# Two memory attentions in a two-block transformer kernel: the root applied to the products, rotary tables computed earlier, latent rounds and weight splits reordered

## The chip, the cores and the metric

The kernel runs on one core of one Trainium2 chip. The metric is the device time of one execution in microseconds, from the hardware's own counters; lower is better. Before the change it takes 3033.23 us (median of 3 runs, 3032.83 to 3034.36).

## What is computed

512 tokens of width 1024 in float32 pass through a first block (state-space, gated recurrence and retention mixers, then a feed-forward) and a second block of two layers. The change touches three parts of the second block, cut here to what matters:

```python
def memory_attention(q_mem, mem, mem_norm_g, w_mem_kv, g_q, g_k):
    q = rms_norm(q_mem.reshape(b, s, MEM_HEADS, MEM_HEAD_DIM), g_q)
    k, v = jnp.split(rms_norm(mem, mem_norm_g) @ w_mem_kv, 2, axis=-1)
    k = rms_norm(k.reshape(b, m, MEM_HEADS, MEM_HEAD_DIM), g_k)
    ...
def mla_queries(h, w_in, g_q_lora, w_uq, g_q_nope, g_q_rope, cos, sin):
    ...
    q = (rms_norm(c_q, g_q_lora) @ w_uq).reshape(b, s, MLA_HEADS, QK_HEAD_DIM)
    q_nope = rms_norm(q[..., :QK_NOPE_DIM], g_q_nope)
    q_rope = apply_rope(rms_norm(q[..., QK_NOPE_DIM:], g_q_rope), cos, sin)
```

The queries of the second layer (the latent attention) are shown; its keys are normed and turned likewise. `rms_norm(mem, g) @ w` is (mem * g * root) @ w with one reciprocal root for each of the 256 memory tokens, so the root can also multiply the product. `cos` and `sin` depend on `positions` alone.

## The kernel before

**Tiling.** Activations lie transposed, 128 channels by 512 tokens to a tile. Weights come as a stream of panels of 128 x 1024 float32 (8 blocks of 128 x 128) in the fixed order of `weight_stream`. Each float32 value is split into a high and a low half; `three` (L661 to L665) makes each block product of three matmuls: high by high, low by high, high by low. A full panel is 24 matmuls of 512 columns; a panel on the 256 memory tokens is 24 of 256 columns.

**Who does what.** SyncE loads panels into four slots `raw`. ScalarE (ACT) makes the high half `w_hi` (L1343). VectorE (DVE, L1850) or, in the panel ranges `POOL_RUNS`, GpSimd (POOL, L622) makes the low half `w_lo`. There are two slots each of `w_hi` and `w_lo`, so the split of panel n+2 starts when panel n is done. Products land in four PSUM banks in turn and are drained by ACT (L1348) or by DVE (`scaled`, L1923); four more (AUX) serve the small steps.

**Order.** Each engine has its own hand-written list; semaphores join them. A waiting instruction holds up all behind it on its engine. The places of the change:

- *First layer* (`conv0`, `qm0`, `conv1`, `mem0`, `conv`): a short convolution of 18 panels with the memory attention woven in. DVE squares and sums the memory tokens (`memory_squares`, L1905 and L1906), multiplies gain and root in and splits (`memory_input`, L2503, L1855, L1856); ACT drains the four `mem0` products. DVE's list ends the stretch with three `w_lo` in a row, and does a part of the convolution (`conv_part(st, 3, 1, 3)`) before the norms of keys and queries.
- *Second layer, latent part* (`mla_in`, `ukv`, `uq`): the heads are normed in rounds of three tiles. A round r is: squares (ACT, L1391), `round_sums` (PE, L796), root (ACT, L1396), reciprocal (DVE, L2023), `round_spread` (PE, L808), three norms (DVE, L2028). Between them stand the `uq` products (`uq_gemm`), four panels for the memory (`mem1_gemm`), turned values (`v_turned_tiles`, L1209) and the rotary turn (`turn`, L2653 to L2655). DVE computes the angle and both rotary tables (L2623 to L2633) between `mla_in` and `ukv`; ACT then takes their sine.
- *Attention steps*: scores, maxima, exponentials, probabilities and values, two steps ahead, from `pair_scores(0)` on.

## Time and profile before

| | us |
|---|---|
| median of 3 runs | 3033.23 (3032.83 to 3034.36) |
| the profiled execution | 3031.66 |
| its span, first to last instruction | 3029.8 |
| PE busy | 2986.1 (99%) |
| DVE busy | 1831.4 (60%) |
| ACT busy | 944.1 (31%) |
| POOL busy | 233.0 (8%) |
| mean granted clock of TensorE | 0.995 |

The trace gives each instruction a start and a duration. Matmuls overlap, so a matmul's own duration says little; the distance from one start to the next is what it costs. In brackets stands how long the engine sat idle before a row and what ended the wait.

### The profile page before, as it was taken

How to read it: one execution, taken by the hardware profiler on the slowest of the kernel's cores; microseconds unless marked ns; L12 is line 12 of the kernel's file. 1: busy time of each engine (PE TensorE's matmuls, PEld its weight loads, DVE VectorE, ACT ScalarE, POOL GpSimd, SP SyncE). 2: the span in 40 equal slices, each digit the busy share in tenths (PEclk: the TensorE clock that was granted, in tenths of full speed). 3: DMA queues.
4: the chain of work that ended last, by engine and by line, in shares of the span. 5: the costliest groups of instructions: out<-in, count | busy, mean ns of one | idle time of the engine just before them, and what ended most of it. 6: DMA issues, size and time to landing. Idle time of an engine off the chain costs nothing.

```text
span 3029.8 us, 36196 instructions
## 1 busy us (share of the span) xinstructions
PE 2986.1 (99%) x13373; PEld 2419.6 (80%) x13373; DVE 1831.4 (60%) x2405; ACT 944.1 (31%) x1279; POOL 233.0 (8%) x107
## 2 busy tenths in 40 slices
PE   8999999999999999999999999999999998999999
PEld 7788788788888888888787888888888875688887
DVE  8896565667766556554577655446554477665532
ACT  4643642333222223222223322222222235322222
POOL 0043340000000000000032000003000022000000
PEclk9999999999999999999999999999999999999999
DMA  4222123223222322223332222332223321122232
GB/s 147 94 95 84 63 98 118 70 95 114 96 94 96 101 98 92 97 95 104 113 104 71 91 97 97 102 106 98 91 96 104 105 87 63 36 91 97 97 104 97
DMA packets 79305, 287.55 MB, mean 95 GB/s; under 512 B 8992, under 2 KB 9248, under 8 KB 78816
## 3 DMA queue, kind: packets, MB, share of 16 engines
q1 hardware_dynamic: 77904, 280.06, 27.8%
q0 software_dynamic: 1296, 6.03, 0.6%
q8 instruction: 73, 1.20, 0.2%
q14 instruction: 32, 0.26, 0.0%
HBM read 283.96 MB, written 2.10 MB: 94 GB/s over the span
## 4 chain that ended last, share of the span: by engine, by line
PE 84%; issue 10%; DVE 4%; POOL 2%; ACT 0%; DMA 0%; POOLq 0%; ACTq 0%
PE ps L663 26%; PE ps L665 26%; PE ps L664 26%; POOL w_lo L622 2%; PE ps L1051 1%; PE ps L1296 0%; PE ps L1259 0%; DVE w_lo L1850 0%; PE ps L832 0%; PE ps L726 0%; PE ps L840 0%; PE ps L1040 0%; ACT w_hi L1343 0%; PE ps L946 0%; PE ps L1262 0%
## 5 line engine op out<-in xcount | busy, mean ns | idle before, releaser
L1343 ACT ACTIVATE w_hi<-raw 128x1024 fp32r<-128x1024 f32 x524 | 554.5, 1058 | 1381.8 <-PE ps L665 1379.7
L663 PE MATMUL ps<-h_hi,w_hi 128*128 128x512 f32 (+1 forms) x2379 | 935.6, 393 | 6.7 <-issue 2.0
L665 PE MATMUL ps<-h_hi,w_lo 128*128 128x512 f32 (+1 forms) x2379 | 924.3, 389 | 0.0
L664 PE MATMUL ps<-h_lo,w_hi 128*128 128x512 f32 (+1 forms) x2379 | 924.2, 388 | 0.0
L1850 DVE TENSOR_TENSOR w_lo<-raw,w_hi 128x1024 fp32r<-128x1024 f32 x434 | 530.7, 1223 | 474.7 <-ACT w_hi L1343 474.1
L663 PEld LDWEIGHTS ps<-h_hi,w_hi 128*128 128x128 f32 x2379 | 448.0, 188 | 113.3 <-issue 12.2
L664 PEld LDWEIGHTS ps<-h_lo,w_hi 128*128 128x128 f32 x2379 | 448.1, 188 | 93.2 <-issue 2.9
L665 PEld LDWEIGHTS ps<-h_hi,w_lo 128*128 128x128 f32 x2379 | 447.7, 188 | 92.7
L663 PE MATMUL ps<-mid_hi,w_hi 128*128 128x512 f32 x1208 | 470.6, 390 | 0.1
L665 PE MATMUL ps<-mid_hi,w_lo 128*128 128x512 f32 x1208 | 470.0, 389 | 0.0
L664 PE MATMUL ps<-mid_lo,w_hi 128*128 128x512 f32 x1208 | 469.9, 389 | 0.0
L622 POOL TENSOR_TENSOR w_lo<-raw,w_hi 128x1024 fp32r<-128x1024 f32 x90 | 225.7, 2508 | 934.4 <-ACT w_hi L1343 926.8
L663 PEld LDWEIGHTS ps<-mid_hi,w_hi 128*128 128x128 f32 x1208 | 226.7, 188 | 48.2 <-DVE mid_lo L1928 0.5
L664 PEld LDWEIGHTS ps<-mid_lo,w_hi 128*128 128x128 f32 x1208 | 226.7, 188 | 47.4 <-issue 0.2
L665 PEld LDWEIGHTS ps<-mid_hi,w_lo 128*128 128x128 f32 x1208 | 226.7, 188 | 47.0
L1923 DVE TENSOR_TENSOR stage<-ps,rstd 128x512 f32<-128x512 f32 x104 | 71.8, 691 | 220.4 <-PE ps L665 220.4
L1348 ACT ACTIVATE stage<-ps 128x512 f32<-128x512 f32 x107 | 63.6, 598 | 365.9 <-PE ps L665 352.9
L663 PE MATMUL ps<-br_hi,w_hi 128*128 128x512 f32 x256 | 101.8, 398 | 9.9 <-DVE br_lo L2064 7.8
L1923 DVE TENSOR_TENSOR tmp<-ps,rstd 128x512 f32<-128x512 f32 x73 | 50.4, 691 | 89.8 <-PE ps L665 89.6
L664 PE MATMUL ps<-br_lo,w_hi 128*128 128x512 f32 x256 | 100.7, 394 | 0.0
L665 PE MATMUL ps<-br_hi,w_lo 128*128 128x512 f32 x256 | 100.6, 393 | 0.0
L1672 ACT ACTIVATE tmp<-tmp 128x512 f32<-128x512 f32 x112 | 69.3, 619 | 63.4 <-DVE tmp L1946 55.4
(409 smaller groups left out, 2478.5 us busy)
## 6 DMA issues: line engine op xcount, KB each, us to landing
raw<-in_wstream SPq DMA_DIRECT2D x525, 512.0 KB, 3.3
x<-in_x SPq DMA_DIRECT2D x4, 512.0 KB, 6.2
x_in<-in_x POOLq DMA_DIRECT2D x8, 256.0 KB, 3.2
mem_x<-in_mem POOLq DMA_DIRECT2D x2, 1024.0 KB, 5.0
out<-x SPq DMA_DIRECT2D x8, 256.0 KB, 4.6
tmp<-in_ret_decay POOLq DMA_DIRECT2D x1, 1024.0 KB, 5.0
rope_r<-in_rope_r POOLq DMA_DIRECT2D x1, 512.0 KB, 3.7
mats<-in_mats SPq DMA_DIRECT2D x1, 256.0 KB, 8.1
```

Of the source, the lines that this page charges most:

```text
L622: nc.gpsimd.tensor_tensor(w_lo[:, n % HL], raw[:, n % RAW], w_hi[:, n % HL].bitcast(F32), ALU.subtract)\
L663: nc.tensor.matmul(dst, hi_w, hi_x, start=first, stop=False)
L664: nc.tensor.matmul(dst, hi_w, lo_x, start=False, stop=False)
L665: return nc.tensor.matmul(dst, lo_w, hi_x, start=False, stop=last)
L1051: mm = nc.tensor.matmul(bank(t)[:, P * c:S], v_tok[:, c, f:f + P], scores[:, hd % 2, OFF[c]:OFF[c] + WIDTH[c]], start=c == 0, stop=True, s ...
L1343: nc.scalar.activation(w_hi[:, n % HL], raw[:, r], ACT.Copy).then_inc(hi_ready, 1)
L1348: nc.scalar.activation(dst, src[rows, 0:cols], func, bias=bias, scale=scale).then_inc(drained, 1)
L1672: nc.scalar.activation(tmp[:, s % 2], tmp[:, s % 2], func).then_inc(act_done, 1)
L1850: v.tensor_tensor(w_lo[:, n % HL], raw[:, n % RAW], w_hi[:, n % HL].bitcast(F32), ALU.subtract)\
L1923: v.tensor_tensor(dst, bank(t), scale, ALU.mult).then_inc(drained, 1)
```

## The change

1. **Root behind the products.** ACT squares the memory in one instruction and makes its high halves with the gain alone (`memory_hi`); DVE sums by one reduction (`memory_sum`) and makes only the low halves (`memory_lo`). The root multiplies the products: in `mem0` as DVE drains them (`memory_drain`), in the second layer by a step on DVE behind ACT's drain (`memory_scaled`).
2. **Rotary tables** are computed on DVE inside `s0b_out` (the output of the first layer's second feed-forward), their sine on ACT behind `s1a_in0`; POOL loads the positions before.
3. **Latent rounds in another order**: the two memory key panels come first in `uq`, sums and spreads stand elsewhere between the products, and the sums of `cq` move ahead by two panels and their spread by one. The weight stream follows.
4. **High halves called sooner**: ACT's `split` of later panels stands ahead of drains and squares it stood behind. Low halves of `uq` panels 1 and 6 go from POOL to DVE.
5. In the first layer the norms of queries and keys come before `conv_part(st, 3, 1, 3)` on DVE.

```diff
-             "mla": (ST["mla_in"].n + 2, ST["wo1"].n)}
+             "mla": (ST["mla_in"].n + 2, ST["uq"].n), "uq": (ST["uq"].n + 2, ST["uq"].n + 5),
+             "wo1": (ST["uq"].n + 7, ST["wo1"].n)}
...
-MEM1_PANEL, MEM1_TILE = (2, 3, 7, 8), (10, 11, 17, 18)
...
+MEM1_PANEL, MEM1_TILE = (0, 1, 7, 8), (2, 3, 17, 18)
...
+            pool.dma_start(krope[:, 0].bitcast(I32), A["positions"].to_broadcast([P, S])).then_inc(side_loaded, 16)
             split_run("s1a")
             pool.wait_ge(posted, ST["s1a_out"].s + 8)
+            pool.wait_ge(side_loaded, 64)
             pool.dma_start(mem_x1[:], A["mem"]).then_inc(side_loaded, 16)
-            pool.wait_ge(side_loaded, 64)
-            pool.dma_start(rope2[:, 0].bitcast(I32), A["positions"].to_broadcast([P, S])).then_inc(side_loaded, 16)
             pool.wait_ge(side_loaded, 80)
             split_run("mla")
+            split_run("uq")
+            split_run("wo1")
...
+                if j == 3:
+                    sums("cq")
...
                 if g == 0:
-                    sums("cq")
-                if g == 1:
                     spread_norms("cq")
...
             v_turned_tiles(0)
-            uq_gemm(0)
+            mem1_gemm(0)
+            mem1_gemm(1)
             round_spread(1)
             round_sums(2)
+            uq_gemm(0)
             v_turned_tiles(2)
+            round_spread(2)
+            round_sums(3)
             uq_gemm(1)
-            round_spread(2)
             v_turned_tiles(4)
-            mem1_gemm(0)
-            mem1_gemm(1)
+            round_spread(3)
+            turn(krope[:, 0])
             uq_gemm(2)
-            round_sums(3)
+            uq_gemm(4)
+            round_sums(4)
             uq_gemm(3)
-            round_spread(3)
-            round_sums(4)
-            uq_gemm(4)
             round_spread(4)
             round_sums(5)
-            turn(krope[:, 0])
             mem1_gemm(2)
+            normalised(4)
+            turn(q_rope[:, 0])
             round_spread(5)
             round_sums(6)
-            normalised(4)
-            turn(q_rope[:, 0])
             mem1_gemm(3)
-            round_spread(6)
-            memory_turned(st.t + MEM1_TILE[2] + 1, mem_vt1, 0)
...
             pe.wait_ge(drained, ST["wo1"].t)
+            normalised(3)
             pair_scores(0)
             pair_scores(1)
-            memory_turned(st.t + MEM1_TILE[3] + 1, mem_vt1, 1)
+            round_spread(6)
+            for j in range(2):
+                memory_turned(mem_vt1, j, (mem_scaled, 3 + j))
             for j in range(1, MLA_HEADS // 2):
                 turn(q_rope[:, j])
...
+                if n == ST["conv0"].n + 2:
+                    act.wait_ge(side_loaded, 48)
+                    nc.scalar.activation(mem_squares, mem_x[:], ACT.Square).then_inc(mem_squared, 1)
+                if n == ST["conv0"].n + 3:
+                    memory_hi(0, mem_x, mem_hi)
...
-            def memory(l, k, v_in):
-
-                st = ST[f"mem{l}"]
-                for j in range(4):
-                    split(st.n + j + 1)
-                    if j == 0:
-                        act.wait_ge(drained, st.t)
-                    drain(st.n + j, st.t + j, k[:, j] if j < 2 else v_in[:, j - 2], cols=MEM)
...
+            for j in range(4):
+                split(ST["mem0"].n + j + 1)
             act.wait_ge(drained, ST["mem0"].t + 2)
             round_squares(0, qm[:, 0], qm[:, 1], mem_k_whole)
...
             silus("s1a_in0", lambda: root_and_split("s1a_in0"))
+            act.wait_ge(sin_in, 2)
+            nc.scalar.activation(rope2, rope2, ACT.Sin).then_inc(sin_done, 1)
...
+            roots("cq")
+            aux[0] += 1
...
                 if g == 0:
+                    act.wait_ge(side_loaded, 80)
+                    act.wait_ge(panel_done, st.n)
+                    memory_hi(1, mem_x1, mem1_hi)
...
+                    if g == 2 and m == 1:
+                        split(ST["uq"].n + 1)
...
             aux[0] += 3
+            v_copies(0)
+            mem1_drain(0)
+            split(st.n + 2)
             act.wait_ge(drained, st.t)
             round_squares(2, *(k_nope[:, hd] for hd in range(3, 6)))
-            v_copies(0)
-            uq_drain(0)
+            mem1_drain(1)
             round_root(2)
             aux[0] += 3
+            split(st.n + 3)
+            act.wait_ge(mem_scaled, 2)
+            round_squares(3, qm[:, 0], qm[:, 1], mem_k1_whole)
+            uq_drain(0)
+            split(st.n + 4)
             v_copies(2)
+            round_root(3)
+            aux[0] += 4
             act.wait_ge(h_ready, 5 * DT)
             uq_drain(1)
+            split(st.n + 5)
             v_copies(4)
-            mem1_drain(0)
...
+                square_of_round(4, j, q_rope[:, j])
+            drain(st.n + UQ_PANEL[2], st.t + UQ_TILE[4], q_rope[:, 2])
+            split(st.n + 6)
...
+            square_of_round(4, 2, q_rope[:, 2])
+            uq_drain(2, 1)
+            uq_drain(4)
...
+            split(st.n + 7)
...
+            uq_drain(3)
+            split(st.n + 8)
...
             mem1_drain(2)
+            split(st.n + 9)
...
                             split(st.n + c * parts + part + 2, i, 4 * parts)
+                            if during:
+                                during(c, part)
...
+            def memory_sum():
+                dve.wait_ge(mem_squared, 1)
+                v.tensor_reduce(acc[:, 0:MEM], mem_squares.rearrange("p k n -> p n k"), AX.X, ALU.add).then_inc(acc_ready, 1)
...
-            def memory_input(l, mem, r, hi, lo, tiles):
-
+            def memory_lo(l, mem, hi, lo, tiles):
                 for k in tiles:
-                    h = acc[:, MEM * (k % 2):MEM * (k % 2) + MEM]
-                    done(v.scalar_tensor_tensor(out=h, in0=mem[:, k], scalar=vcol("mem_norm_g_2", 8 * l + k),
-                                                in1=r[:, 0:MEM], op0=ALU.mult, op1=ALU.mult))
-                    halves(hi[:, k], lo[:, k], h, h_ready)
+                    dve.wait_ge(mem_cast, 8 * l + k + 1)
+                    v.scalar_tensor_tensor(out=lo[:, k], in0=mem[:, k], scalar=vcol("mem_norm_g_2", 8 * l + k),
+                                           in1=hi[:, k].bitcast(F32), op0=ALU.mult, op1=ALU.subtract).then_inc(h_ready, 1)
+
+            def memory_drain(j):
+                st = ST["mem0"]
+                dve.wait_ge(panel_done, st.n + j + 1)
+                dst = mem_k[:, j] if j < 2 else mem_vt[:, j - 2]
+                v.tensor_tensor(dst, bank(st.t + j)[:, 0:MEM], mem_root, ALU.mult).then_inc(drained, 1)
...
+            def memory_scaled(j):
+                dve.wait_ge(drained, ST["uq"].t + MEM1_TILE[j] + 1)
+                tile = mem_k1[:, j] if j < 2 else mem_vt1[:, j - 2]
+                v.tensor_tensor(tile, tile, mem_root, ALU.mult).then_inc(mem_scaled, 1)
...
-            memory_squares(48, mem_x, 5)
+            memory_sum()
...
-            memory_rms(r)
-            memory_input(0, mem_x, r, mem_hi, mem_lo, range(0, 4))
+            memory_rms()
+            memory_lo(0, mem_x, mem_hi, mem_lo, range(0, 4))
             conv_part(ST["conv1"], 2, 0, 2)
-            memory_input(0, mem_x, r, mem_hi, mem_lo, range(4, 8))
+            memory_lo(0, mem_x, mem_hi, mem_lo, range(4, 8))
             conv_part(ST["conv1"], 2, 1, 2)
             split(ST["mem0"].n + 1)
             conv_part(ST["conv1"], 2, 2, 2)
+            memory_drain(0)
             for j in range(1, 4):
                 split(ST["mem0"].n + j + 1)
+                memory_drain(j)
...
-            conv_part(st, 3, 1, 3)
             round_norms(*memory_gain("q", 0), qm[:, 0], qm[:, 1])
             round_norms(*memory_gain("k", 0), mem_k_whole)
+            conv_part(st, 3, 1, 3)
...
+            def rotary_rest(part, quarter):
+                done(v.scalar_tensor_tensor(out=part, in0=turns, scalar=-c1, in1=angle, op0=ALU.mult, op1=ALU.add))
...
+                v.tensor_scalar(part, part, -3.1415925, None, ALU.max).then_inc(sin_in, 1)
+
+            def rotary_tables(c, part):
+                if (c, part) == (1, 0):
+                    rotary_angle()
+                    rotary_turns(0.25)
+                if (c, part) == (1, 1):
+                    rotary_rest(rope2[:, 0], 0.25)
+                if (c, part) == (2, 0):
...
+            ffn("s0b", gain2(1, 0), during=rotary_tables)
...
+            reciprocals("cq")
...
-            memory_input(1, mem_x1, spare[:, 0], mem1_hi, mem1_lo, range(0, 4))
+            memory_lo(1, mem_x1, mem1_hi, mem1_lo, range(0, 4))
...
+            memory_lo(1, mem_x1, mem1_hi, mem1_lo, range(4, 8))
+            split(ST["uq"].n + 1)
             round_reciprocal(1)
-            memory_input(1, mem_x1, spare[:, 0], mem1_hi, mem1_lo, range(4, 8))
             round_norms(gk, *(k_nope[:, hd] for hd in range(3)))
+            for j in range(2):
+                memory_scaled(j)
             round_reciprocal(2)
             round_norms(gk, *(k_nope[:, hd] for hd in range(3, 6)))
             round_reciprocal(3)
             round_norms(*memory_gain("q", 1), qm[:, 0], qm[:, 1])
             round_norms(*memory_gain("k", 1), mem_k1_whole)
+            dve.wait_ge(sin_done, 1)
+            turn(krope[:, 0])
+            split(ST["uq"].n + 6)
             round_reciprocal(4)
             round_norms(gr, *(q_rope[:, j] for j in range(3)))
             round_reciprocal(5)
-            dve.wait_ge(sin_done, 1)
-            turn(krope[:, 0])
+            turn(q_rope[:, 0])
             round_norms(gq, *(q_nope[:, hd] for hd in range(3)))
+            memory_scaled(2)
             round_reciprocal(6)
-            turn(q_rope[:, 0])
-            round_norms(gq, *(q_nope[:, hd] for hd in range(3, 6)))
```

How the orders move at three places:

DVE at the end of `mem0` and the start of `conv`, before (`spare` holds the root; `ckv` the rows of a round):

```order
L1850 TENSOR_TENSOR w_lo<-raw,w_hi 128x1024 [waits hi_ready] x3
L1923 TENSOR_TENSOR tmp<-ps,rstd 128x512 [waits panel_done]
L2023 RECIPROCAL ckv<-ckv 96x512 [waits rows_rooted]
L2509 COPY mem_v<-ps 128x2x128 [waits aux_done] x2
L1923 TENSOR_TENSOR stage<-ps,rstd 128x512 [waits panel_done]
L2530 TENSOR_TENSOR cpad<-tmp,stage 128x512 [waits drained]
L1942 TENSOR_SCALAR tmp<-cpad,vec 128x512 [waits dve_step]
L1946 SCALAR_TENSOR_TENSOR tmp<-cpad,vec,tmp 128x512 [waits dve_step] x2
L2028 SCALAR_TENSOR_TENSOR qm<-qm,vec,ps 128x512 [waits aux_done,dve_step]
L2028 SCALAR_TENSOR_TENSOR qm<-qm,vec,ps 128x512 [waits aux_done]
L2028 SCALAR_TENSOR_TENSOR mem_k<-mem_k,vec,ps 128x512 [waits aux_done]
```

and with the change:

```order
L2535 TENSOR_TENSOR mem_vt<-ps,spare 128x256 [waits panel_done]
L1877 TENSOR_TENSOR w_lo<-raw,w_hi 128x1024 [waits hi_ready]
L2535 TENSOR_TENSOR mem_vt<-ps,spare 128x256 [waits panel_done]
L1952 TENSOR_TENSOR tmp<-ps,rstd 128x512 [waits panel_done]
L2052 RECIPROCAL ckv<-ckv 96x512 [waits rows_rooted]
L2544 COPY mem_v<-ps 128x2x128 [waits aux_done] x2
L2057 SCALAR_TENSOR_TENSOR qm<-qm,vec,ps 128x512 [waits aux_done] x2
L2057 SCALAR_TENSOR_TENSOR mem_k<-mem_k,vec,ps 128x512 [waits aux_done]
L1952 TENSOR_TENSOR stage<-ps,rstd 128x512 [waits panel_done]
L2565 TENSOR_TENSOR cpad<-tmp,stage 128x512 [waits drained]
L1971 TENSOR_SCALAR tmp<-cpad,vec 128x512 [waits dve_step]
```

The `w_lo` are no longer three in a row, the products `mem_k` and `mem_vt` are drained by DVE between them, and the norms (the rows on `qm` and `mem_k` with `vec`) stand right behind the copies.

PE behind the last product of `uq`, before (scores of the memory on `qm`):

```order
L808 MATMUL ps<-ckv,mats 128x512 [waits rms_done,aux_used]
L808 MATMUL ps<-ckv,mats 128x512 x2
L1100 MATMUL ps<-mats,rstd 128x128 [waits rms_done,aux_used,drained]
L1100 MATMUL ps<-mats,rstd 128x128
L821 MATMUL ps<-spare,qm 128x256 [waits drained]
L821 MATMUL ps<-spare,qm 128x256 x7
L1100 MATMUL ps<-mats,rstd 128x128 [waits rms_done,aux_used,drained]
L1100 MATMUL ps<-mats,rstd 128x128
L1201 MATMUL ps<-q_rope,mats 128x512 [waits rms_done,aux_used] x2
```

and with the change:

```order
L831 MATMUL ps<-mem_k,qm 128x256 [waits aux_used,drained]
L831 MATMUL ps<-mem_k,qm 128x256 x7
L818 MATMUL ps<-ckv,mats 128x512 [waits rms_done,aux_used]
L818 MATMUL ps<-ckv,mats 128x512 x2
L1110 MATMUL ps<-mats,rstd 128x128 [waits rms_done,aux_used,mem_scaled]
L1110 MATMUL ps<-mats,rstd 128x128
L1110 MATMUL ps<-mats,rstd 128x128 [waits rms_done,aux_used,mem_scaled]
L1110 MATMUL ps<-mats,rstd 128x128
L1211 MATMUL ps<-q_rope,mats 128x512 [waits rms_done,aux_used] x2
```

The scores of the first two steps come ahead of the last spread (the rows on `ckv`), and both turnings of the memory's values behind it.

DVE in the last rounds, before:

```order
L2653 TENSOR_TENSOR ps<-ps,rope 128x512 [waits aux_done,sin_done]
L2654 TENSOR_TENSOR krope<-krope,rope 128x512 [waits dve_step]
L2655 TENSOR_TENSOR krope<-krope,ps 128x512 [waits dve_step]
L2028 SCALAR_TENSOR_TENSOR q_nope<-q_nope,vec,ps 128x512 [waits aux_done] x3
L2023 RECIPROCAL ckv<-ckv 96x512 [waits rows_rooted]
L2653 TENSOR_TENSOR ps<-ps,rope 128x512 [waits aux_done]
L2654 TENSOR_TENSOR q_rope<-q_rope,rope 128x512 [waits dve_step]
L2655 TENSOR_TENSOR q_rope<-q_rope,ps 128x512 [waits dve_step]
L2028 SCALAR_TENSOR_TENSOR q_nope<-q_nope,vec,ps 128x512 [waits aux_done] x3
L2509 COPY spare<-ps 128x2x128 [waits aux_done]
L2001 TENSOR_REDUCE small<-ps 128x2 [waits mem_scored]
L2003 TENSOR_SCALAR small<-small 128x2 [waits dve_step]
```

and with the change:

```order
L2052 RECIPROCAL ckv<-ckv 96x512 [waits rows_rooted]
L2697 TENSOR_TENSOR ps<-ps,cpad 128x512 [waits aux_done]
L2698 TENSOR_TENSOR q_rope<-q_rope,cpad 128x512 [waits dve_step]
L2699 TENSOR_TENSOR q_rope<-q_rope,ps 128x512 [waits dve_step]
L2057 SCALAR_TENSOR_TENSOR q_nope<-q_nope,vec,ps 128x512 [waits aux_done] x3
L2540 TENSOR_TENSOR rstd<-rstd,spare 128x256 [waits drained]
L2052 RECIPROCAL ckv<-ckv 96x512 [waits rows_rooted]
L2030 TENSOR_REDUCE small<-ps 128x2 [waits mem_scored]
L2032 TENSOR_SCALAR small<-small 128x2 [waits dve_step]
L2030 TENSOR_REDUCE small<-ps 128x2 [waits mem_scored]
L2032 TENSOR_SCALAR small<-small 128x2 [waits dve_step]
L2540 TENSOR_TENSOR rstd<-rstd,spare 128x256 [waits drained]
```

The last three norms stand behind the first maxima (TENSOR_REDUCE), the turn of `q_rope` ahead of the norms of `q_nope`, and one product of the root (`rstd` by `spare`) ahead of the last reciprocal.

## Rows read from the trace of the kernel before

**Rows 1.** The page, busy time of each engine.
```profile
PE 2986.1 (99%) x13373; PEld 2419.6 (80%) x13373; DVE 1831.4 (60%) x2405; ACT 944.1 (31%) x1279; POOL 233.0 (8%) x107
```
**Rows 2.** Waits of PE: for whom, us in total, times, longest.
```profile
PE ps L808 <- DVE ckv L2023: 6.2, 3, 3.6
PE ps L663 <- DVE w_lo L1850: 4.6, 4, 2.8
```
**Rows 3.** Windows: stretch, length; busy us (count) of each engine, PEclk, DMA share, GB/s.
```profile
1561.60:1578.90 17.30, 14.49 (x98) 14.27 (x96) 11.55 (x16) 5.05 (x7) 0.00 (x0) 0.80 0.36 117
...
2488.80:2556.80 68.00, 56.62 (x313) 36.88 (x313) 49.94 (x57) 36.35 (x63) 22.45 (x10) 0.95 0.24 78
```
**Rows 4.** Timeline of PE in the latent part: start, us, instruction, idle before.
```profile
2441.64 0.63 PE L665 MATMUL ps<-h_hi,w_lo 128*128 128x512 f32 x1
2442.07 0.63 PE L663 MATMUL ps<-h_hi,w_hi 128*128 128x512 f32 x1
...
2455.40 0.39 PE L663 MATMUL ps<-h_hi,w_hi 128*128 128x512 f32 x1
2455.63 0.39 PE L664 MATMUL ps<-h_lo,w_hi 128*128 128x512 f32 x1
```
**Rows 5.** Groups by line of DVE from 1520 to 1565 us, the memory's.
```profile
L1905 DVE TENSOR_TENSOR stage<-mem_x 128x256 f32<-128x256 f32 x8 | 5.6, 703 | 0.3
L1856 DVE TENSOR_TENSOR mem_lo<-acc,mem_hi 128x256 fp32r<-128x256 f32 x8 | 5.5, 684 | 0.3
L1855 DVE CAST mem_hi<-acc 128x256 fp32r<-128x256 f32 x8 | 4.4, 553 | 0.3
L2503 DVE SCALAR_TENSOR_TENSOR acc<-mem_x,vec,spare 128x256 f32<-128x256 f32 x8 | 3.9, 490 | 0.0
```
**Rows 6.** The page's costliest groups, high and low half of a weight panel's split.
```profile
L1343 ACT ACTIVATE w_hi<-raw 128x1024 fp32r<-128x1024 f32 x524 | 554.5, 1058 | 1381.8 <-PE ps L665 1379.7
...
L1850 DVE TENSOR_TENSOR w_lo<-raw,w_hi 128x1024 fp32r<-128x1024 f32 x434 | 530.7, 1223 | 474.7 <-ACT w_hi L1343 474.1
```
**Rows 7.** Timeline of PE in `mem0` and behind.
```profile
1567.45 0.58 PE L663 MATMUL ps<-mem_hi,w_hi 128*128 128x256 f32 x1 [2.81 <-DVE w_lo L1850]
...
1576.01 0.28 PE L663 MATMUL ps<-mem_hi,w_hi 128*128 128x256 f32 x1
...
1578.89 0.47 PE L663 MATMUL ps<-h_hi,w_hi 128*128 128x512 f32 x1
...
1599.35 1.13 PE L821 MATMUL ps<-mem_k,qm 64*128 64x256 f32 x8 [3.75 <-DVE mem_k L2028]
```
**Rows 8.** Timeline of DVE in the first layer.
```profile
1569.83 1.22 DVE L1850 TENSOR_TENSOR w_lo<-raw,w_hi 128x1024 fp32r<-128x1024 f32 x1
...
1597.23 1.41 DVE L2028 SCALAR_TENSOR_TENSOR qm<-qm,vec,ps 128x512 f32<-128x512 f32 x2
```
**Rows 9.** Timeline of DVE in the latent part.
```profile
2492.66 3.34 DVE L2023 RECIPROCAL ckv<-ckv 96x512 f32<-96x512 f32 x1
...
2509.22 2.06 DVE L2028 SCALAR_TENSOR_TENSOR k_nope<-k_nope,vec,ps 128x512 f32<-128x512 f32 x3 [1.30 <-PE ps L808]
...
2524.64 3.35 DVE L2023 RECIPROCAL ckv<-ckv 96x512 f32<-96x512 f32 x1 [13.35 <-ACT ckv L1396]
...
2542.11 1.51 DVE L2654 TENSOR_TENSOR krope<-krope,rope 128x512 f32<-128x512 f32 x1
...
2550.20 0.69 DVE L2654 TENSOR_TENSOR q_rope<-q_rope,rope 128x512 f32<-128x512 f32 x1
...
2555.82 0.17 DVE L2009 RECIPROCAL small<-small 128x2 f32<-128x2 f32 x1
```
**Rows 10.** Timeline of ACT, root and squares of a round.
```profile
2491.88 0.68 ACT L1396 ACTIVATE ckv<-ps,small 96x512 f32<-96x512 f32 x1
2492.47 1.66 ACT L1391 ACTIVATE tmp<-k_nope 128x512 f32<-128x512 f32 x3
```
**Rows 11.** Timeline of POOL, the split beside L2654's first row.
```profile
2540.69 2.38 POOL L622 TENSOR_TENSOR w_lo<-raw,w_hi 128x1024 fp32r<-128x1024 f32 x1 [4.71 <-ACT w_hi L1343]
```

140 lines of the change are left out of this document (61 added, 79 removed).

## The prediction

> **What bounds the kernel.** First the page's busy times: PE is busy 99% of the span [rows 1], so time can only be won where PE waits or runs below its full clock. Next the waits of PE by releaser [rows 2]: they are short, and the largest stand on DVE, which is where the change works. Then windows, which place them [rows 3]: in `mem0`, 1561.6 to 1578.9, the granted clock is 0.80; in the latent rounds, 2488.8 to 2556.8, PE does 56.6 us in 68.0 at a clock of 0.95. Last the timelines. At full clock two matmuls of 512 columns start 0.23 apart, at half clock, 1.2 GHz in place of 2.4, 0.43 apart [rows 4]. So there are two stretches to work out, everything else being back to back.
>
> I add against the profiled execution, 3031.66 us, whose span is 3029.8 with 1.9 around it. The median of the runs is 1.6 above it, which I add at the end.
>
> **First layer.** Removed on DVE before `mem0`: 8 squares of 703 ns and 8 sums alike, 11.2 us [rows 5]; and of the three steps to a tile of memory input (490, 553 and 684 ns, 13.8 us for 8 tiles) one stays, at 490 ns. Added: one reduction of 2048 elements, which no row shows. Four times the 0.7 us of a row on 512 elements is 2.8; from below, the two reads of the present way could be no cheaper than a quarter of 11.2, also 2.8; I take 2.8 and it is covered, since DVE then waits for PE. ACT gets one square of 2048 elements, twice the 1.06 us of a 1024 element row [rows 6], and 8 short casts in another panel, each in a gap: a panel takes 5.4 us (24 times 0.227), and between the end of panel n and the start of n+2 stand one cast of 1.06 and one subtraction of 1.22 on DVE [rows 6] or 2.38 on POOL [rows 11], 3.6 in all with the handovers. If a gap fails by x, PE waits x.
>
> With DVE on time, the `w_lo` of `mem0`'s second panel is ready about 1564.2 in place of 1567.4. A panel of 256 columns takes 2.7 to 2.9 (the last one, 1576.01 to 1578.89 [rows 7]), while its split needs 1.06 + 1.22 plus a drain on DVE of 0.4 (over half of the 0.69 that 512 elements take [rows 9]), and behind the second one also four steps of the convolution, 2.5 by the same measure. I walk DVE's list: drain at 1567.2, `w_lo` of the third panel at 1568.5 (now it starts 1569.83 [rows 8]), where PE would need it at 1567.05. So a wait of 1.5 replaces one of 2.81 [rows 7]; the others vanish. `mem0` ends about 1574.1 plus 0.5 for a short spell of half clock, 1574.6 against 1578.89 [rows 7]: **4.3 won**.
>
> Next is the wait of 3.75 before the scores at 1599.35 [rows 7]. The norms start at 1597.23 [rows 8] because `conv_part(st, 3, 1, 3)` stands before them. Behind the spread they take 2.1 (three of 0.69, as in rows 9). By the walk spread, half a panel and scores follow one another without a wait: the wait of 3.75 goes, so do, as I estimate, 0.3 of slow start before it and 1.6 of half clock behind it (8 products at twice 0.2). What is late next is the convolution step: it pushes the first maxima to about 4 us behind the scores, exponentials end about 5 us behind, and PE asks for them 5.6 us behind (two half panels). Just covered, I charge 0.4. **5.2 won**, 9.5 in the first layer, with ends of 7 (the cover fails) and 10.5.
>
> **Rotary tables.** Their 16 steps leave DVE's list ahead of `cq`. They go into four panels of `s0b_out`, at most five steps at a place, each no longer than 0.69, so up to 3.4 us, beside one `w_lo` of 1.22 in a panel of 5.4, with POOL at rest: no cost; were the gap missed, each place would cost under 1. The sine (1024 elements, so 1.06 by the row on `w_hi` [rows 6]) goes behind a product's drain, the order showing no table load with it. POOL's second DMA goes with its handover, hidden either way.
>
> **Latent rounds.** What this frees is lateness of DVE: `cq` is split and ready about 2485 in place of 2492.7, and eight memory steps of three become eight of one. The sums of `cq` cost PE the same at their new place; but the third `ukv` product no longer has a spread before it to cover ACT's first drain: a wait of 0.8. From 2488.8 I walk the new order with a reciprocal of 3.34 and three norms of 2.06 [rows 9], a root of 0.68 and three squares of 1.66 [rows 10], sums and spread of 1.0 to 1.1 each on PE (three or more products of 0.23 and their start), 4.1 for two `uq` tiles (18 times 0.227) and 2.7 for a memory panel. A round's serial part is root, reciprocal, spread and norms: 0.7 + 3.3 + 1.1 + 2.1, about 7.2.
>
> The starts I get on PE are: first memory panel 2491.6 (0.8 waiting for drains), both 1.4 longer for half clock, spread 1 at 2498.5, spread 2 at 2506.0, spread 3 at 2513.1, spread 4 at 2526.4, spread 5 at 2533.0 (waits 1.3 for its reciprocal). Behind it the turn of `q_rope` on DVE holds the AUX bank that the last sums need. L2654 took 1.51 when POOL's `w_lo` ran (it ends at 2543.07 [rows 11], L2654 at 2543.62), against 0.69 alone [rows 9]; here the split of `wo1`'s first panel falls on it, so the turn ends at 2536.9 in place of 2535.1. The last sums follow, the fourth memory panel with 0.8 of half clock, then scores from 2541.4, spread 6 at 2543.9 and the first probability on DVE at 2548.1, where now it stands at 2555.82 [rows 9]. From there on both orders do the same steps: **7.7 won, less about 0.2**, so 7.5. Ends: no blocked turn and no half clock give 11.3; one more blocked step (2.3) and PE slow for another 10 us (2 to 3) give 3.
>
> For the blocked step the Trainium skill (SBUF — State Buffer, Two separate sides) has a rule: the second of two instructions wanting the port shared by DVE and GpSimd blocks until the first is done, also for a DVE step with two SBUF inputs. By that rule, the trace agrees on L2654; it speaks against this change once more, since `memory_scaled` reads two SBUF operands and stands within 0.5 us of POOL's split of `uq` panel 3: the sum by it would be 2.3 worse.
>
> **Sum.** 3031.66 − 9.5 − 7.5 = 3014.7 by the profile; with the 1.6, **3016**.
>
> **The rivals.**
> - *The rounds win nothing.* DVE stays the last in every round, and each wait only moves from one reciprocal to the next. For it: three of the present waits are for L2023 [rows 2] and the chain of 7.2 is untouched. Against it: DVE does only 49.9 in 68.0 [rows 3], with the largest hole (13.35 at the third round [rows 9]) because the round's squares come late, which the order mends. It leaves the first layer: 3033.2 − 9.5 = 3023.7.
> - *Everything fits.* No block, no half clock, cover everywhere: 10.5 + 11.3, 3011.4. For it: my walk is charged with events that hang on some tenths.
> - *Gains fall below what can be told.* The splits on DVE wait behind reciprocals or the first maxima come late: 3028 or more, under 6 us won.
> - *Half clock through the rounds, slower.* If the new order breaks PE's work into short pieces with waits between, the stretch could stay at 1.2 GHz. Place: the `uq` part; price: 81 matmuls of 512 columns at 0.20 more and 96 of 256 at 0.10 more, 25.8. That gives 3016 + 25.8 = 3042. It decides against the change once more than about 17 us, two thirds of the products, run slow. Against it: the rows now show a clock of 0.95 over this stretch [rows 3] with longer waits in it. The Trainium skill (TensorE: Matmul & The Clock Gate, What's actually happening) says that the slow state is the default and activity releases it; on rows 4, behind a run of tiny matmuls, the trace agrees. That the changed kernel does not do what it says I rule out from its order.
>
> **Chances.** Forecast 0.60 (its own range 3012 to 3021), all fits 0.17, rounds win nothing 0.15, gain too small 0.05, slower 0.03. Measurement tells about 0.2%, 6 us, from no change. Faster by more than that: 0.60 + 0.17 + 0.15 = 0.92; within it 0.05; slower 0.03. The range of 8 in 10 takes in most of the second and third case: 3010 to 3026.
>
> **What would show it.** In `mem0` one wait on `w_lo` of 1 to 2 us and a clock over 0.9; scores of the first layer with no wait on `mem_k`, about 9 us earlier; in the latent part the first step on `neg_r` some 7 us nearer to `ukv`'s end, waits on L2052 (the reciprocal) under 3 us in total, and one on the last turn. Wrong would be: a PE wait above 1 us in `s0b_out`, a score of the first layer waiting for exponentials, the clock of the rounds under 0.9, or waits for ACT's squares in every round.

## The result, and the profile after

The changed kernel takes 3015.32 us (median of 4 runs, 3014.54 to 3015.93) against 3033.03 for the kernel before in the same runs: ratio 0.9943, 95% interval 0.9931 to 0.9956. (The ratios here and below are those on record; the quotient of the two medians can differ from them in the fourth place, here 0.9942.) The forecast was 3016 in a range of 3010 to 3026. The profiled execution took 3015.93 with a span of 3014.1, where before it was 3031.66 and 3029.8: 15.7 less. Of all executions behind this document one, of old_both, took 8155.77 us and is left out of that kernel's median.

The page, busy time by engine, answers to [rows 1]:

```profile
PE 2982.4 (99%) x13373; PEld 2417.7 (80%) x13373; DVE 1815.6 (60%) x2367; ACT 948.3 (31%) x1290; POOL 228.3 (8%) x105
```

PE issues as many matmuls as before and is busy 3.7 less; DVE does 38 steps and 16 us less. Four of the waits of PE (for whom, us in total, times, longest) answer to [rows 2]:

```profile
PE ps L673 <- POOL w_lo L629: 2.6, 4, 1.2
PE ps L673 <- DVE w_lo L1877: 2.5, 4, 0.8
PE ps L806 <- DVE q_rope L2699: 2.4, 1, 2.4
...
PE ps L818 <- DVE ckv L2052: 0.7, 1, 0.7
```

The reciprocals of the rounds held PE for 6.2 in three waits; now it is 0.7 in one. The new wait is the 2.4 for the turn of `q_rope`. Windows over the two stretches and one more answer to [rows 3]:

```profile
1560.80:1573.30 12.50, 11.73 (x97) 11.51 (x96) 8.61 (x12) 5.76 (x7) 0.00 (x0) 1.00 0.49 162
2478.20:2539.00 60.80, 55.65 (x314) 37.01 (x314) 44.27 (x45) 34.91 (x62) 16.76 (x7) 0.94 0.27 87
2599.60:2603.50 3.90, 3.88 (x15) 3.46 (x16) 0.30 (x1) 2.48 (x4) 0.00 (x0) 0.57 0.00 0
```

`mem0` went from 17.3 us at a clock of 0.80 to 12.5 at 1.00. The rounds went from 68.0 to 60.8 at nearly the same clock, 0.95 and 0.94. The third window, a stretch at half clock inside the attention, comes up again in the last section. PE's timeline at the places that matter (start, us, instruction, idle before) answers to [rows 7] and, from 2472.59 on, goes through the latent part:

```profile
1567.49 0.39 PE L673 MATMUL ps<-mem_hi,w_hi 128*128 128x256 f32 x1 [0.77 <-DVE w_lo L1877]
...
1573.34 0.40 PE L673 MATMUL ps<-h_hi,w_hi 128*128 128x512 f32 x1
...
1589.93 1.14 PE L831 MATMUL ps<-mem_k,qm 64*128 64x256 f32 x8
...
2472.59 0.47 PE L673 MATMUL ps<-lat_hi,w_hi 128*128 128x512 f32 x1 [0.78 <-ACT k_nope L1359]
...
2521.91 1.13 PE L818 MATMUL ps<-ckv,mats 32*128 32x512 f32 x6 [0.72 <-DVE ckv L2052]
2525.44 1.93 PE L806 MATMUL ps<-tmp,mats 128*32 128x512 f32 x6 [2.40 <-DVE q_rope L2699]
2532.63 2.00 PE L831 MATMUL ps<-mem_k,qm 64*128 64x256 f32 x16 [0.47 <-ACT rstd L1359]
...
2539.01 0.61 PE L1267 MATMUL ps<-k_nope,q_nope 128*128 128x128 f32 x4
```

The first row stood at a wait of 2.81, the third at one of 3.75.

**Where the 15.7 are.** Differences between the starts of the same rows on PE, one profile of each kernel. `mem0` runs from its first product to the first of `conv`; "scores" from there to the first scores of the memory (L831); "first layer's rest" from there to the first product on `cat_hi`; "to ukv's end" from the first short sums (128 x 1, L771 in the changed kernel) at the end of the second feed-forward to the first sums behind `ukv`; "rounds" from there to the first product of keys and queries (L1267); "attention" from there to the last group of products on `p_tok` and `v_mla`.

| | mem0 | scores | first layer's rest | to ukv's end | rounds | attention |
|---|---|---|---|---|---|---|
| before | 17.28 | 20.46 | 49.57 | 50.81 | 68.07 | 62.40 |
| changed | 12.53 | 16.59 | 47.99 | 51.27 | 60.77 | 64.48 |
| changed_again | 12.54 | 16.59 | 47.99 | 51.26 | 60.88 | 64.36 |
| norms_late | 12.54 | 20.41 | 50.56 | 51.28 | 60.91 | 64.35 |
| input_heavy | 16.65 | 16.60 | 47.98 | 49.66 | 59.53 | 63.16 |
| rotary_back | 12.54 | 16.60 | 47.98 | 51.95 | 60.70 | 64.32 |
| lat_heavy | 12.53 | 16.60 | 47.98 | 51.97 | 66.23 | 64.32 |
| old_rounds | 12.53 | 16.59 | 47.99 | 51.24 | 64.05 | 62.41 |
| old_both | 12.54 | 16.59 | 47.99 | 50.38 | 66.58 | 61.43 |
| splits_late | 12.54 | 16.59 | 47.99 | 51.29 | 58.42 | 64.02 |
| uq_on_pool | 12.53 | 16.59 | 47.99 | 51.27 | 61.60 | 64.45 |
| wo1_on_dve | 12.54 | 16.59 | 47.99 | 51.28 | 58.38 | 62.32 |
| panel_ahead | 12.53 | 16.59 | 47.99 | 51.21 | 59.38 | 62.32 |
| tail_and_cq | 12.54 | 16.59 | 47.99 | 51.28 | 56.48 | 61.80 |

From before to changed: 4.75 + 3.87 + 1.58 − 0.46 + 7.30 − 2.08 = 14.96. The rest, 0.8, lies ahead of `mem0`, 0.7 of it between 12 and 15 us of the span, where nothing was changed: the matmuls' starts go from 0.43 apart to 0.23 at 12.2 us in the changed kernel and at 13.9 before. What stands outside these stretches agrees within 0.1 (789.04 and 789.05 between the first layer and the end of the second feed-forward, with the rotary tables in it). The table is read by column: an edit shows where it acts, and stretches ahead of it repeat within 0.1, which no median of whole runs does. Stretches behind an edit are less firm. input_heavy changes neither code nor waits in the rounds and is 1.24 shorter there, all of it in one panel behind the same wait of 2.40 (4.11 for 5.33), by the clock.

### The profile page after: what moved, and what is told of

The parts are those of the page before. It is cut to its first block, busy times and chain, and to the rows that moved or that the text cites. A ratio compares the mean times of both kernels' runs of the same rounds, so it can differ in the third digit from the quotient of the medians.

```text
span 3014.1 us, 36095 instructions
## 1 busy us (share of the span) xinstructions
PE 2982.4 (99%) x13373; PEld 2417.7 (80%) x13373; DVE 1815.6 (60%) x2367; ACT 948.3 (31%) x1290; POOL 228.3 (8%) x105
## 4 chain that ended last, share of the span: by engine, by line
PE 87%; issue 8%; DVE 3%; POOL 1%; ACT 0%; DMA 0%; POOLq 0%; ACTq 0%; DVEq 0%
PE ps L673 27%; PE ps L675 27%; PE ps L674 27%; POOL w_lo L629 1%; PE ps L1061 1%; PE ps L1267 0%; PE ps L1304 0%; DVE w_lo L1877 0%; PE ps L842 0%; ACT w_hi L1354 0%; PE ps L1050 0%; PE ps L736 0%; PE ps L1270 0%; PE ps L956 0%; PE ps L850 0%
## 5 line engine op out<-in xcount | busy, mean ns | idle before, releaser
L1952 DVE TENSOR_TENSOR tmp<-ps,rstd 128x512 f32<-128x512 f32 x73 | 50.4, 691 | 89.9 <-PE ps L675 89.8
```

What stands on the lines that cost most here:

```text
L1952: v.tensor_tensor(dst, bank(t), scale, ALU.mult).then_inc(drained, 1)
```

## The experiments

### What held mem0 (input_heavy)

```diff
 def memory_lo(l, mem, hi, lo, tiles):
     for k in tiles:
         dve.wait_ge(mem_cast, 8 * l + k + 1)
+        if l == 0:
+            done(v.scalar_tensor_tensor(out=acc[:, 0:MEM], in0=mem[:, k], scalar=vcol("mem_norm_g_2", k),
+                                        in1=mem_root, op0=ALU.mult, op1=ALU.mult))
+            done(v.tensor_copy(acc[:, MEM:2 * MEM].bitcast(F32R), acc[:, 0:MEM]))
```

> The changed kernel, but DVE makes the two steps per tile of memory input again whose results nobody reads (a multiplication by gain and root and a cast, 8 times each, about 0.49 and 0.55 us, 8.3 us in all), everything else as in the changed kernel. Theory 'what delayed mem0 was the length of DVE's list': idle DVE before the first w_lo of mem0 is 0.85 + 1.02 + 1.13 = 3.0 us in the changed kernel, so that w_lo comes 4 to 5 us later; PE waits about 1 for the low halves, 3 to 4 for this w_lo and 1 for the next one: 4.0 to 6.5 us slower than the changed kernel, the whole gain of mem0 (4.75) or more. Rival 'what helped is the order inside mem0, a drain between two w_lo in place of three w_lo in a row': under 1 us slower.

Measured: 3018.29 us, ratio 0.9955 (0.9941 to 0.9968). `mem0` takes 16.65, 4.12 more. PE's timeline of this kernel:

```profile
1567.46 0.39 PE L673 MATMUL ps<-mem_hi,w_hi 128*128 128x256 f32 x1 [3.39 <-DVE w_lo L1877]
```

The order inside `mem0` was the new one, drains between the `w_lo`, and the wait came back all the same, 0.6 larger than before. So the length of DVE's list ahead of `mem0` decided. With that larger wait `mem0` is still 0.6 shorter than before, so 1.2 are due to something else. That the interleaving earns them is not shown: behind the wait, from 1567.4 to 1573.5 us, the granted clock was 0.50 before and 0.72 here. In this profile the 4.1 were given back in three columns that the edit does not touch, 1.6 in "to ukv's end", 1.2 in the rounds and 1.3 in the attention, by the clock: it is the lowest of the five executions, 3016.13, and the highest took 3020.07.

### What held the first scores (norms_late)

```diff
-round_norms(*memory_gain("q", 0), qm[:, 0], qm[:, 1])
-round_norms(*memory_gain("k", 0), mem_k_whole)
 conv_part(st, 3, 1, 3)
+round_norms(*memory_gain("q", 0), qm[:, 0], qm[:, 1])
+round_norms(*memory_gain("k", 0), mem_k_whole)
```

> The changed kernel with conv_part(st, 3, 1, 3) back ahead of the norms of queries and keys on DVE. Theory 'DVE's order holds the scores' (the prediction's): in the changed kernel the norms start at 1587.12, right behind the spread, and the scores at 1589.93 wait for nothing. With the step back in front (its product is ready about 1586.1, five steps of 0.69 to 1.54, 3.5 in all) the norms start at 1589.6 and end at 1591.7, so PE waits 1.7 before the scores and runs up to 1.6 at half clock behind: 1.7 to 3.3 us slower than the changed kernel. Rival 'the scores came earlier only because mem0 did': the norms move with the rest, no wait, within 0.5 us.

Measured: 3022.62, ratio 0.9965 (0.9951 to 0.9979). The first scores come 3.82 later, the rest of the layer costs 2.57 more: 6.4, twice the top of what was expected. DVE and PE of this kernel, two views:

```profile
1587.88 2.50 DVE L1971 TENSOR_SCALAR tmp<-cpad,vec 128x512 f32<-128x512 f32 x1
...
1591.99 1.41 DVE L2057 SCALAR_TENSOR_TENSOR qm<-qm,vec,ps 128x512 f32<-128x512 f32 x2
```
```profile
1594.11 2.08 PE L831 MATMUL ps<-mem_k,qm 64*128 64x256 f32 x8 [3.75 <-DVE mem_k L2057]
```

The wait is that of before to the hundredth. I had costed the convolution's steps at their free length; L1971 takes 0.49 alone and here 2.50, beside a split on POOL (2587.62 to 2590.10). The block of 2.0 is the difference between the 1.7 expected and the 3.75 measured. Behind the wait the scores take 2.0 for 1.1 and the next 24 products 7.3 for 5.7, at half clock, which is the 2.57. Before the change the same wait had the slow products behind it but not the slow scores (1.1): again the clock, 0.9 this time.

### The rotary tables (rotary_back), and both loads (lat_heavy)

The tables' 14 last steps move back behind `split(ST["ukv"].n + 1)`, the sine behind the second `ukv` product. `lat_heavy` adds to that the two steps of `input_heavy`, for `l == 1`.

> The changed kernel with 14 of the 16 steps of the rotary tables back between mla_in and the memory's low halves (the angle stays in s0b_out), and the sine behind the second ukv product's drains. Theory 'the tables made DVE late for the latent rounds': they take 12 to 13 us there, DVE now has idle 5.13 + 0.93 + 1.26 before cq's split, of which some is used, so the second half of the memory's low halves ends about 5 us later than 2477.6, PE waits 3 to 5 before the first memory panel and the first reciprocal starts about 5 us later: 4 to 7 us slower than the changed kernel. Rival 'the rounds are a chain of their own and the tables were covered' : under 1 us.

> The kernel with the rotary tables moved back (0.8 us slower than the changed one in that stretch), and DVE makes for each of the second layer's eight memory tiles two steps more whose results nobody reads (0.49 and 0.29 to 0.55 us each as rows show, 6 to 8 us in all). Theory 'DVE had idle time for one of the two loads, not for both': in the run with the tables moved back DVE has no idle time left from 2460.7 to 2488.5, so the low halves for the first memory panel and the first reciprocal come 6 to 8 us later: 5 to 9 us slower than the run with the tables moved back. Rival 'the rounds have their own slack': under 2 us.

Measured: rotary_back 3015.55, ratio 0.9946 (0.9933 to 0.996); lat_heavy 3023.39, ratio 0.997 (0.9958 to 0.9982). The tables cost 0.7 ahead of the rounds and nothing in them: the rival was right. Of the 0.7, 0.63 is a wait of PE for ACT's squares. It is the sine that delays them, and not the steps on DVE: at this place it comes with a load of ACT's table before it and one before the next root, and the kernel before has the same two.

```profile
2474.76 1.28 ACT L1777 ACT_TABLE_LOAD   x1
2476.06 1.06 ACT L1777 ACTIVATE cpad<-cpad 128x1024 f32<-128x1024 f32 x1
...
2482.53 1.28 ACT L1407 ACT_TABLE_LOAD   x1
```
```profile
2479.77 0.59 PE L806 MATMUL ps<-tmp,mats 128*32 128x512 f32 x1 [0.63 <-ACT stage L1402]
```

The changed kernel has 47 such loads, the kernel before and rotary_back 49: behind `s1a_in0` the sine needs none of its own. This gain of the move is on ACT and was in no term of the prediction. DVE was late (the first reciprocal starts at 2485.14, 2.3 later than in the changed kernel once both are counted from `mem0`), but it now has two memory panels on PE in front of it, and the four-tile groups of low halves took 1.67 each, as POOL's splits fell elsewhere, and not the 3.45 and 3.81 I had read in the changed kernel. With both loads the cover is used up: 5.53 more in the rounds than rotary_back. PE of lat_heavy, one of four such waits in the first memory panels:

```profile
2484.98 0.39 PE L673 MATMUL ps<-h_hi,w_hi 128*128 128x256 f32 x1 [1.49 <-DVE h_lo L2533]
```

### The order of the rounds (old_rounds), and with the tables back (old_both)

`old_rounds` takes from the kernel before: `MEM1_PANEL`, `UQ_PANEL`, `V_TILE`, the weight stream, the lists of PE, ACT and DVE for `uq`, and POOL's ranges; `memory_scaled` stands ahead of the norms that read its tiles. `old_both` adds the move of `rotary_back`.

> The changed kernel with the latent rounds, the weight stream, ACT's splits and POOL's share as before the change; the root behind the products, the early rotary tables, the earlier sums of cq and the first layer stay changed. Theory A 'the new order of rounds and splits is what wins': all the 6.8 us that the stretch from ukv to the first scores gained come back less what the freed DVE gives (cq ready some 8 us earlier than before, which takes away the 1.99 and part of the 3.58 wait): 3 to 6 us slower than the changed kernel. Theory B 'less work for DVE is what wins, order does not matter': within 1 us of the changed kernel.

> The kernel with the rounds in the old order (64.05 from ukv's end to the first key and query product, 68.07 before the change, 60.77 with it), and the 14 steps of the rotary tables back ahead of the memory's low halves. It tells to which part of DVE's relief the 4.0 go. Theory A 'to the tables, in this order': cq's halves end beside 2483 in place of some 2475, and as uq's products on cq come first here, PE waits 2 to 3.5 and each round shifts: 2 to 4 us slower than with the old rounds alone. Theory B 'to the memory's input, one step for three': with the new rounds the tables cost 0.7, and here too under 1 us.

Measured: old_rounds 3017.8, ratio 0.9954 (0.994 to 0.9967), rounds 64.05, 3.28 more than changed; old_both 3019.52, ratio 0.996 (0.9947 to 0.9972), rounds 66.58, 2.53 more again. PE's waits in old_rounds show three for reciprocals, as before:

```profile
PE ps L670 <- POOL w_lo L628: 4.8, 6, 1.3
PE ps L815 <- DVE ckv L2035: 4.4, 3, 2.2
```

The 2.53 of old_both have two parts. 1.07 stand at once, since `cq`'s last low half ends later and the first `uq` product waits for it. The other 1.45 come behind a wait for a reciprocal that both kernels have, 2.17 and 2.16: in old_both PE is at half clock behind it and in old_rounds not. So of the 7.30 in the rounds 3.3 are the order with its splits, 1.1 the tables and 1.4 the clock; the remaining 1.5 would be the memory's input and the earlier sums of `cq`, but no run takes these alone, and each part is uncertain by about the 1.2 that the clock took from the rounds of input_heavy. The split also depends on the path: in the new order the tables are worth nothing in the rounds. Each part makes room that the other could also have used.

### Splits called sooner (splits_late, uq_on_pool)

```diff
-mem1_drain(0)
-split(st.n + 2)
+split(st.n + 1)
+mem1_drain(0)
...
-split(st.n + 9)
 round_root(6)
+split(st.n + 9)
 mem1_drain(3)
```

and for `uq_on_pool` the range `"mla"` goes to `ST["wo1"].n`, and DVE's two `split` in the rounds are gone.

> The changed kernel with only ACT's splits of uq's panels back where they were called before (that of panel n + 1 ahead of the drains of panel n, in place of n + 2 behind them), the order of the rounds stays new. Theory 'the early call matters': w_hi of uq panel 1 comes at about 2484 in place of 2480.4, DVE's split of it stands ahead of the first reciprocal, which starts 3 us later, and POOL's low halves of the next panels (2.4 each) end 1 to 2 us behind the time at which PE wants them: 3 to 8 us slower than the changed kernel. Rival 'the chain of reciprocals sets the rounds and splits hide in it': under 1 us.

> The changed kernel with the low halves of uq panels 1 and 6 on POOL as before the change. Theory 'POOL's 2.4 against DVE's 1.2 decides at panel 6': its high half is ready at 2509.2, the low half at 2511.7, PE wants it at 2510.9 and waits 0.8, a little half clock behind: 0.5 to 1.5 us slower than the changed kernel. Rival 'a step of DVE is blocked beside POOL's longer split': at panel 1 only a step behind 2480.4 could be, the reciprocal there does not stretch in any row; with a block in the turn of krope or the norms, 1.7 more. Third, no effect: within 0.5.

Measured: splits_late 3013.95, ratio 0.9941 (0.9927 to 0.9954), and uq_on_pool 3016.92, ratio 0.9946 (0.9933 to 0.9959). The second came as expected: one wait of 0.77 for POOL at panel 6, rounds 0.8 longer. The first fell the other way: its rounds are 2.35 shorter. Up to the fourth spread it is 1.4 later (38.36 behind `ukv`'s end, 36.94 in the changed kernel), with two waits for `w_lo`:

```profile
2484.50 0.39 PE L673 MATMUL ps<-h_hi,w_hi 128*128 128x256 f32 x1 [1.01 <-DVE w_lo L1876]
...
2512.57 0.50 PE L673 MATMUL ps<-h_hi,w_hi 128*128 128x512 f32 x1 [1.01 <-DVE w_lo L1876]
...
2526.00 1.06 PE L806 MATMUL ps<-tmp,mats 128*32 128x512 f32 x6 [1.22 <-DVE q_rope L2698]
```

Then it gains more than that. Late splits also put that of `wo1`'s first panel behind the last root, so POOL makes its low half from 2528.82 on, off the turn; the turn is stretched only a little, by the split of the panel before (its middle step takes 1.21). So the experiment undid two things, one that helps a little and one that harms more. The rival, that splits hide in the chain of reciprocals, does not hold either: 1.4 is more than the 1 it allowed.

### The blocked step (wo1_on_dve)

```diff
-             "wo1": (ST["uq"].n + 7, ST["wo1"].n)}
+             "wo1": (ST["uq"].n + 7, ST["wo1"].n - 1)}
...
 round_reciprocal(6)
+split(ST["wo1"].n)
```

> The changed kernel, with the low half of wo1's first panel made by DVE behind the last reciprocal (idle for 2.31 there) and not by POOL at 2521.78 to 2524.12. Theory 'one blocked step on DVE holds the last sums': L2698 at 2522.28 took 2.38 beside this split and 0.69 elsewhere, and the last sums waited 2.40 for the turn; unblocked, sums, root, reciprocal and spread 6 come 1.7 earlier and less of the fourth memory panel runs at half clock: 1.5 to 3.5 us faster than the changed kernel. Rival 'something else is late next' (the reciprocal of round 5, the norms): under 0.5 us.

Measured: 3011.11, ratio 0.9929 (0.9916 to 0.9943). Changed kernel, DVE and POOL around the turn:

```profile
2521.58 0.67 DVE L2697 TENSOR_TENSOR ps<-ps,cpad 128x512 f32<-128x512 f32 x1
2522.28 2.38 DVE L2698 TENSOR_TENSOR q_rope<-q_rope,cpad 128x512 f32<-128x512 f32 x1
```
```profile
2521.78 2.34 POOL L629 TENSOR_TENSOR w_lo<-raw,w_hi 128x1024 fp32r<-128x1024 f32 x1 [1.97 <-ACT w_hi L1354]
```

wo1_on_dve, DVE and PE:

```profile
2522.44 0.69 DVE L2698 TENSOR_TENSOR q_rope<-q_rope,cpad 128x512 f32<-128x512 f32 x1
```
```profile
2523.91 1.06 PE L806 MATMUL ps<-tmp,mats 128*32 128x512 f32 x6 [0.71 <-DVE q_rope L2699]
```

The wait falls from 2.40 to 0.71, the sums behind it from 1.86 to 0.99 and the memory panel behind them from 5.33 to 3.61, since less of it runs at half clock: the last spread comes 4.3 earlier after `ukv`'s end (52.04 for 56.32). In this pair of profiles one blocked step cost 4.3, though the block itself is 1.7. The part that is half clock varies: behind the same wait of 2.40 sums and panel took 7.2 in the changed kernel and 6.0 in input_heavy, beside 4.6 here, so the block costs between 3.1 and 4.3. Not all of it reaches the end of the rounds, which are 2.39 shorter: the split, now on DVE between the last reciprocal and the maxima, makes a new wait of 1.25 for `rstd` (L2540). The median is 4.2 under that of the changed kernel, and in the profile 2.16 of the gain lie in the attention, which the edit does not touch; the last section says why these can't be credited to it.

L2697 began 0.20 ahead of POOL, has an operand in PSUM and kept its 0.67; L2698 has both in SBUF, began behind POOL's start and ended 0.54 behind its end. By the rule of the Trainium skill (SBUF — State Buffer, Two separate sides) that the earlier of two such instructions keeps the shared port until it is done, the trace agrees. The same section of the Trainium skill adds that DVE in a fast mode takes that port too. L1971 agrees: it has one input, and in norms_late it was stretched to 2.50; alone it takes 0.49, where steps of the same size with two inputs take 0.69. No run shows the mode itself.

### The tail in another order (panel_ahead, tail_and_cq)

```diff
+mem1_gemm(3)
 round_spread(5)
 round_sums(6)
-mem1_gemm(3)
```

with `mem1_drain(3)` ahead of the last root, on top of wo1_on_dve, save that `split(ST["wo1"].n)` moves from behind the last reciprocal into the attention; `tail_and_cq` keeps the order of PE there and has, on DVE,

```diff
+memory_scaled(3)
 pair_max(0, 0)
 pair_max(0, 1)
-memory_scaled(3)
```

the same `split` inside the attention, `spread_norms("cq")` behind the second `ukv` product, and all low halves of the memory ahead of those of `cq`.

> The kernel with the low half of wo1's first panel on DVE (made later here, inside the attention), and the fourth memory panel ahead of the fifth spread and the last sums on PE, its drain ahead of the last root on ACT. Theory 'in the tail PE waits for a chain that has slack elsewhere': with the panel in between, the waits for the fifth reciprocal (0.72), for the turn (2.40 in the changed kernel) and the half clock on that panel (2.6) go, and the last spread waits about 2.5 for its reciprocal instead: scores 5 us earlier, last spread 3 to 4 earlier, 2.5 to 5 us faster than the changed kernel and 0 to 2.5 faster than the run with wo1's panel on DVE alone. Rival 'maxima and probabilities, which stand behind the last reciprocal on DVE, set what follows': no faster than that run.

> The kernel with the low half of wo1's first panel on DVE, three changes more: that half is made inside the attention and not ahead of the first maxima; the fourth memory product's root ahead of the maxima; cq's spread one ukv panel later, with all low halves of the memory ahead of cq's on DVE. Theory 'each small wait goes by its own': the wait for the first drain of the third ukv product (0.78, with 0.9 of half clock around it) goes, maxima start 0.7 earlier and the wait of 1.25 for rstd goes: 1 to 2.5 us faster than with wo1's panel on DVE alone. Rival 'the steps behind on DVE take it back': within 0.7 us.

Measured: panel_ahead 3013.28, ratio 0.9937 (0.9923 to 0.995), rounds 1.0 longer than wo1_on_dve. The scores do come 2.3 earlier, but the fifth norms wait for a spread that now stands behind a panel, and the last reciprocal waits behind these norms on DVE:

```profile
2531.64 1.13 PE L818 MATMUL ps<-ckv,mats 32*128 32x512 f32 x6 [2.82 <-DVE ckv L2052]
```

So neither theory as it stood: it is not the maxima, but the chain has no slack before the last reciprocal.

tail_and_cq takes 3009.72, ratio 0.9925 (0.9912 to 0.9937), beside 3016.32 for the changed kernel in the same runs: the fastest here, 22 us under the kernel before (3031.62 in those runs). The rounds are 1.9 shorter than in wo1_on_dve: the maxima start at once behind `rstd`, and the wait of 1.25 is gone. Which of the two moves on DVE did that was not separated. The `cq` part brought nothing: the wait for ACT's first drain only moved to the second product, 0.84 for 0.78, and the stretch stays at 51.28. In all these kernels it is the `ukv` product without another step in front that pays it.

### The changed kernel again (changed_again)

> The changed kernel once more, on the chip and beside the runs of the next three. Theory 'half clock comes and goes with the moment, not with the work': between the first key and query product of the second layer and the last value product the first profile took 64.48, three others of the same work 62.3 to 62.4; a second profile may show either length, and all stretches ahead of it agree within 0.1. Rival 'the 2.1 belong to this order': 64.4 to 64.5 again. Median 3014 to 3017 by both.

Measured: 3016.32, ratio 0.9948 (0.9935 to 0.996). All stretches agree within 0.12, the attention too: 64.36. That looks as if the 2.1 belonged to this order, but the two profiles lose them at different places. Against before, the first profile of the changed kernel is 0.5 late after 15 us of the attention and loses the other 1.6 behind the last wait, at 60.6 us. The second is 2.0 late after 16 us and loses nothing behind that wait. Same kernel, same sum, other places: the sum's repeating does not show that the order causes it.

## Why the prediction held

- **The signs.** The first scores came 9.4 earlier, the first step on `neg_r` 7.4 nearer to `ukv`'s end, waits for reciprocals of the rounds are 0.7 in total, and one wait stands at the last turn, all as said. No wait shows in `s0b_out`: the 789 us around it agree to 0.01.
- **First layer, 9.5 forecast, 10.2 measured.** `mem0`: 4.3 forecast, 4.75 measured. The wait on `w_lo` is 0.77 and not 1.5 and no half clock remains, both charged too high. The reduction of 2048 elements took 3.95 and not 2.8 (L2517 at 1521.68); it was covered, as said. Scores and rest: 5.2 forecast, 3.87 + 1.58 = 5.45; no exponential was late. norms_late and input_heavy show both causes as named.
- **Rotary tables, nothing.** Right for the place where they went. But the sentence that they free DVE's lateness for the rounds was only half right: in the new order their steps could have stayed on DVE at no cost that shows, and the 0.7 of rotary_back is the sine on ACT with its table loads.
- **Rounds, 7.5 forecast, 7.30 − 0.46 = 6.8 measured.** Shifted by the 10.5 that the kernel was ahead at `ukv`'s end, the walk's five spreads, at 2498.5, 2506.0, 2513.1, 2526.4 and 2533.0, stood at 2497.4, 2504.7, 2511.9, 2525.7 and 2532.4. The wait of 0.8 in the third `ukv` product is there, 0.78. So the spreads came 0.6 to 1.3 ahead of the walk: the first two memory panels took 5.9 at full clock, where I had 6.9 up to the first spread. The mis-sized term is the turn. I charged the blocked step with a delay of 1.8, and it was 1.7. But from the last sums to the first scores I had 4.5, with 0.8 of half clock, and it took 7.2: the sums 1.9 in place of 1.0, the panel 5.3 in place of 3.5, 0.47 of it a wait for ACT. The first scores came at 2543.2 so counted, not at 2541.4, and the first probability at 2548.9, not at 2548.1.
- **Not in the sum.** 2.1 lost in the attention and 0.8 won ahead of the first layer's stretch, by the clock at places that the change does not touch. They cancel in part. The profiled execution came out at 3015.93, 1.2 above the sum's 3014.7. The 1.6 between profiled execution and median was taken from the kernel before; here the median lies 0.6 below the profiled execution. That the forecast of the median is off by only 0.7 is luck: its terms do not deserve it.
- **The rivals.** That the rounds win nothing fell: waits for the reciprocals are 0.7 of 6.2. That everything fits fell at the blocked turn; wo1_on_dve, without that block, comes to 3011.1, where this rival had 3011.4, but with 9.2 won in the rounds and `ukv` together, and not 11.3, so the nearness is in part chance. That the gains fall below what can be told fell with 17.7 us won. Half clock through the rounds: the clock stayed at 0.94. The further block that the Trainium skill's rule would have brought for `memory_scaled` did not happen; those two steps were done (2490.02 to 2490.77) before POOL began at 2490.78. A margin of 0.01 is luck and says nothing against the rule.

## What to carry to other kernels

When an engine off the critical path is late, count its list up to the wait and see what cover each order gives it: two reliefs that fill the same gap are not worth their sum. Walk the shared port like a queue: a step of 0.69 that began 0.5 into a split of 2.34 took 2.38, and the half clock behind the wait added 1.4 to 2.6. Moving a function of ACT can add or save a table load, 1.28 each here. An experiment that undoes an early call also moves the last one of its chain; look at what that one lands on.
